# Two FFN weight units multiplied token tile by token tile inside the norm ahead of the FFN

## The reference

```python
        x = x + rms_norm(mix, norm_mix_post[l])
        f = conv_ffn(rms_norm(x, norm_ffn_pre[l]), ffn_up[l], ffn_conv_w[l], ffn_down[l])
        x = x + rms_norm(f, norm_ffn_post[l])
```

## Time and profile before

| what | us |
|---|---|
| median of 3 runs | 2019.67 (2017.91 to 2019.98) |
| profiled execution | 2023.55 |
| its span | 2021.8 |
| PE busy | 1932.9 (96%) |
| DVE busy | 983.6 (49%) |
| ACT busy | 639.9 (32%) |

### The profile page before, as it was taken

How to read it: one execution, slowest core, us unless ns; L and a number is a source line. 1 busy time by engine, 2 the same in 40 slices (tenths; PEclk the granted TensorE clock), 3 DMA queues, 4 the chain that set the end, 5 groups by cost and what they waited for, 6 DMA issues and landing times.

```text
span 2021.8 us, 26669 instructions
## 1 busy us (share of the span) xinstructions
PE 1932.9 (96%) x10902; PEld 1277.9 (63%) x10902; DVE 983.6 (49%) x1678; ACT 639.9 (32%) x1075; POOL 11.4 (1%) x25
## 2 busy tenths in 40 slices
PE   8999999999999999999999999999999899999997
PEld 8979998979998887877996333333333333333332
DVE  6888788888877575488755111111111111111112
ACT  5565556565547333355544000000000000000001
POOL 0000000010000000000000000000000000000000
PEclk9999999999999999999999999999999999999999
DMA  8356654437554640334469999999999999999997
GB/s 336 123 196 221 208 183 178 166 157 260 204 197 153 214 144 34 136 106 166 169 228 363 410 383 434 432 430 432 432 432 432 430 432 432 431 433 431 430 432 304
DMA packets 48225, 592.06 MB, mean 293 GB/s; under 512 B 5696, under 2 KB 6400, under 8 KB 15808
## 3 DMA queue, kind: packets, MB, share of 16 engines
q1 hardware_dynamic: 46080, 584.13, 71.7%
q0 software_dynamic: 1760, 6.33, 1.0%
q10 hardware_dynamic: 288, 0.24, 0.0%
HBM read 589.63 MB, written 1.05 MB: 292 GB/s over the span
## 4 chain that ended last, share of the span: by engine, by line
PE 73%; DMA 19%; DVE 4%; ACT 2%; issue 1%; SPq 0%; DVEq 0%; ACTq 0%
PE psum L2288 46%; PE psum L2737 20%; DMA slots<-exp_w_dram 18%; PE psum L2894 3%; PE psum L2690 3%; DMA work<-exp_w_dram 1%; PE psum L2760 1%; ACT work L1044 0%; DVE work L1609 0%; DMA slots<-w_in_dram 0%; DVE work L1899 0%; DVE split_weights L1554 0%; DVE work L1919 0%; ACT work L1294 0%; DVE split_rows L1514 0%
## 5 line engine op out<-in xcount | busy, mean ns | idle before, releaser
L2737 PE MATMUL psum<-slots,work 128*64 128x512 f32 x2304 | 531.1, 613 | 47.9 <-DMA slots<-exp_w_dram 44.6
L2288 PE MATMUL psum<-split_rows,split_weights 128*128 128x256 f32 (+1 forms) x3888 | 514.1, 294 | 6.7 <-DVE split_rows L1514 3.7
L2288 PEld LDWEIGHTS psum<-split_rows,split_weights 128*128 128x128 f32 x3888 | 493.8, 193 | 28.9 <-issue 9.7
L2737 PEld LDWEIGHTS psum<-slots,work 128*64 128x64 f32 x2304 | 166.3, 140 | 373.5 <-issue 330.4
L2251 DVE TENSOR_SCALAR work<-psum 128x512 f32<-128x512 f32 x32 | 22.1, 692 | 490.9 <-PE psum L2801 490.9
L1535 DVE TENSOR_TENSOR split_weights<-slots,split_weights 128x1024 fp32r<-128x1024 f32 x180 | 219.5, 1223 | 84.6 <-ACT split_weights L1084 83.7
L1084 ACT ACTIVATE split_weights<-slots 128x1024 fp32r<-128x1024 f32 x180 | 190.4, 1062 | 182.3 <-PE psum L2288 161.7
L2288 PE MATMUL psum<-split_weights,split_rows 128*128 128x512 f32 x1008 | 237.0, 395 | 0.0
L2288 PEld LDWEIGHTS psum<-split_weights,split_rows 128*128 128x128 f32 x1008 | 190.1, 190 | 40.9 <-issue 1.7
L1437 ACT ACTIVATE work<-work 128x512 f32<-128x512 f32 x32 | 20.2, 631 | 528.5 <-DVE work L2251 528.5
L2737 PE MATMUL psum<-work 128*64 128x512 f32 x756 | 168.5, 594 | 4.9 <-DMA work<-exp_w_dram 4.7
(11 more groups left out here) (294 smaller groups left out, 1410.0 us busy)
## 6 DMA issues: line engine op xcount, KB each, us to landing
slots<-exp_w_dram SPq DMA_DIRECT2D x65, 4096.0 KB, 29.0
work<-exp_w_dram SPq DMA_DIRECT2D x21, 4096.0 KB, 29.9
slots<-w_in_dram SPq DMA_DIRECT2D x56, 1024.0 KB, 5.1
slots<-ffn_up_dram SPq DMA_DIRECT2D x44, 1024.0 KB, 5.0
cond_work<-ada_wT_dram SPq DMA_DIRECT2D x48, 512.0 KB, 4.4
slots<-ffn_down_dram SPq DMA_DIRECT2D x20, 1024.0 KB, 4.9
slots<-exp_w_dram SPq DMA_DIRECT2D x10, 2048.0 KB, 14.0
slots<-w_out_dram SPq DMA_DIRECT2D x12, 1024.0 KB, 4.8
```

The lines of the kernel that those rows point to most:

```text
L2288: return nc.tensor.matmul(out_, lhsT, rhs, start=first, stop=last)
L2737: return nc.tensor.matmul(b[rows, :], lhs[:, rows], rhs, start=first, stop=last, skip_group_check=True)
```

## The change

In both layers, in the norm ahead of the FFN:

- PE: the five fillers are gone. Between the transposes of tile 0 and of tile 1 stand 24 products of units 24 and 25, for tile 0 alone and the first four k of each unit; behind the transposes of tile 1 come the other 24 of tile 0 and the 48 of tile 1. So 96 products with 128 moving columns take the place of 48 with 256. They wait for the banks of `F` one by one. The unit loop begins with unit 26.
- ACT rounds the rows tile by tile. Three banks of tile 0 are rounded between the two squarings of tile 1, the other five banks after the last root.
- DVE takes the low part of two banks of tile 0 after it added tile 1 to `x` and ahead of its normalising, the other six banks after.
- The wait for the FFN's parameters moves from behind the norm to ahead of it, on both engines.

```diff
@@ -33,6 +33,7 @@
 CAT_AT = XHAT_AT + 2 * 2048
 HALF = 2048
 TILE_ORDER = ((0, 0), (1, 0), (0, 1), (1, 1), (2, 0), (2, 1), (3, 0), (3, 1))
+TILE_BY_TILE = tuple((i, t) for t in range(TT) for i in range(4))
 ROW_SLICES = (4, 5, 6, 7, 8)
 RING = 5
 UNIT = 1024
@@ -1064,9 +1065,9 @@
             def evac(key, l, out_, in_, func=ACT.Copy, **kw):
                 nc.scalar.activation(out_, in_, func, **kw).then_inc(evacuated[bank_of(key)], 1)
 
-            def high_rows(key, l, n, col):
-
-                for i, t in TILE_ORDER:
+            def high_rows(key, l, n, col, order=TILE_ORDER):
+
+                for i, t in order:
                     b = take(act, (key, 4 * t + i), l)
                     for c in (0, 1):
                         k = 2 * i + c
@@ -1170,13 +1171,15 @@
                 nc.scalar.activation(flat(cat_split[:, 0, 2:4, :]), take(act, ("RT", 0), l), ACT.Copy).then_inc(cat_high_ready, 1)
                 split_until(MIX_UNITS + 1)
                 load_root_table()
+                act.wait_ge(ffn_par_loaded, 32 * l + 32)
                 for t in range(TT):
                     for square in (square_of_bank, square_of_sum):
                         square("M", l, t, 0)
                         square("M", l, t, 1)
                         root(t)
-                act.wait_ge(ffn_par_loaded, 32 * l + 32)
-                high_rows("F", l, 4, COL_FFN_PRE)
+                        if t and square is square_of_bank:
+                            high_rows("F", l, 4, COL_FFN_PRE, TILE_BY_TILE[0:3])
+                high_rows("F", l, 4, COL_FFN_PRE, TILE_BY_TILE[3:])
 
                 def first_tap(g, u):
                     if g >= 2 and u == 0:
@@ -1503,9 +1506,9 @@
                                                    in1=x[:, t, cut], op0=ALU.mult, op1=ALU.add
                                                    ).then_inc(evacuated[bank_of((key, 2 * t + half))], 1)
 
-            def low_rows(key, l, n, col):
-
-                for j, (i, t) in enumerate(TILE_ORDER):
+            def low_rows(key, l, n, col, order=TILE_ORDER, begun=0):
+
+                for j, (i, t) in enumerate(order, begun):
                     dve.wait_ge(hT_high_ready, 16 * l + (2 * n + j + 1))
                     b = psum[:, bank_of((key, 4 * t + i)), :]
                     tile = slice(t * P, (t + 1) * P)
@@ -1725,12 +1728,14 @@
                                         cat_split[:, 0, 2:4, :].rearrange("p k t -> p (k t)"), ALU.subtract
                                         ).then_inc(evacuated[bank_of(("RT", 0))], 1)
                 split_until(MIX_UNITS + 1)
+                dve.wait_ge(ffn_par_loaded, 32 * l + 32)
                 for t in range(TT):
                     times_gain("M", mix_row, t, (16 * l + 4 * t + 1, 16 * l + 4 * t + 2))
                     add_to_x(l, 8 * l + 2 * t + 3, "M", t)
+                    if t:
+                        low_rows("F", l, 4, COL_FFN_PRE, TILE_BY_TILE[0:2])
                     normalise_tile(8 * l + 2 * t + 4, t)
-                dve.wait_ge(ffn_par_loaded, 32 * l + 32)
-                low_rows("F", l, 4, COL_FFN_PRE)
+                low_rows("F", l, 4, COL_FFN_PRE, TILE_BY_TILE[2:], 2)
 
                 def later_taps(g, u):
                     b = take(dve, ("U", 2 * g + u), l)
@@ -2995,9 +3000,30 @@
 
                 pe.wait_ge(xhat_tile_ready, 2 * l + 2)
                 turn("F", l, 0)
-                keep_clock(("F", 4), l, 5)
+                first = [[unit_weights(MIX_UNITS + c, v) for v in (0, 1)] for c in (0, 1)]
+
+                def tile_products(c, t, ks):
+
+                    b = psum[:, bank_of(("U", 0)), c * T + t * P:c * T + (t + 1) * P]
+                    for k in ks:
+                        if c == 0 and k % 2 == 0:
+                            after_evacuation(pe, ("F", 4 * t + k // 2), l)
+                        for i, (a, v) in enumerate(PASSES):
+                            ins = nc.tensor.matmul(b, first[c][a][:, k, :], hT_split[:, v, k, t * P:(t + 1) * P],
+                                                   start=c + t + k + i == 0, stop=k == KC - 1 and i == 2,
+                                                   skip_group_check=True)
+                    return ins
+
+                fill(pe, ("U", 0), l)
+                pe.wait_ge(w_split, l * len(UNITS) + MIX_UNITS + 2)
+                for c in (0, 1):
+                    tile_products(c, 0, range(4))
                 pe.wait_ge(xhat_ready, 2 * l + 2)
                 turn("F", l, 1)
+                for c in (0, 1):
+                    tile_products(c, 0, range(4, KC))
+                tile_products(0, 1, range(KC)).then_inc(unit_used, 1)
+                done(tile_products(1, 1, range(KC)), ("U", 0))
                 def context_turned(items):
 
                     pe.wait_ge(ctx_hat_ready, 2)
@@ -3010,7 +3036,7 @@
                                                           ctx_row[:, t, k * P:(k + 1) * P], ident)
                         done(ins, ("CT", i))
 
-                for n in range(MIX_UNITS, len(UNITS) - 2):
+                for n in range(MIX_UNITS + 2, len(UNITS) - 2):
                     slot, j = UNITS[n]
                     kind, g = LAYER_SLOTS[slot]
                     if (l, kind, g) == (DEPTH - 1, "down", 4) and j in (0, 3):
@@ -3022,7 +3048,7 @@
                     if kind == "up":
                         u, c = divmod(j, 2)
                         b = fill(pe, ("U", 2 * g + u), l) if c == 0 else psum[:, bank_of(("U", 2 * g + u)), :]
-                        ins = column_unit(b[:, c * T:(c + 1) * T], wu, "F" if n == MIX_UNITS else None)
+                        ins = column_unit(b[:, c * T:(c + 1) * T], wu)
                         if last:
                             done(ins, ("U", 2 * g + u))
                     else:
```

## The result

The change makes the kernel slower: 2029.03 us (median of 10 runs) against 2017.34 (10 runs), 11.7 us more where 4.6 were forecast. The ratio is 1.0072 with a 95% interval of 1.0045 to 1.0099, that is +9 to +20 us; it goes by the means here, which the highest runs pull up (14.6 us apart). The runs of before lie within 5.3 us. Those of the change lie in three groups: five from 2023.24 to 2025.53, two at 2032.53 and 2034.62, three from 2043.16 to 2044.05. The profiled execution is the one of 2034.62, from the middle group.

The account below looks back on a forecast made before the run. PE was taken as the bound, so unit 26's delay passes on fully: +0.6 us a layer at full clock plus 1.7 for the clock dip, +2.3 a layer, +4.6 in all, median 2024.3 us; range 2017.5 to 2029.4.

Parts of the forecast that it names:

- The steps up to the clock: Layer 0, PE from tile 0's transposes to unit 26 at full clock: 137.96 against 137.37 before, +0.6 us.
- PE's first product: PE behind tile 0's transposes: idle 2.65 us until bank 0's release, first product at 126.46.
- The rows' extra work: ACT and DVE in the norm: tile 1's rows ready about 0.32 us later, but PE is later still, so cost 0.
- The transposes of tile 1: PE, layer 0: they start behind the 24 narrow products, at 129.10 at full clock.
- The narrow product: A 128-column product on PE, set by its weight load: 0.110 us, taken from products with 64 columns.
- The whole sum for full clock: Layer 0, tile 0's transposes to unit 26: 137.96 - 122.72 = 15.24 us.
- The rivals with other prices: Narrow products at stream speed, 0.066 us: -5.5 us in all, chance 0.13; at full 4-byte price, 0.240: +26, chance 0.12.
- the 1.56 us: Kernel before, layer 0: unit 26's delay from an undisturbed 135.81 to 137.37, read as wholly the lowered clock.
- the dip: PE's one idle piece of 2.65 us lowers the clock for 3.4 us, as before: 1.7 us a layer.
- The bound from above: Upper limit on the lowered clock's cost behind PE's gap: 1.7 us a layer.
- the prediction's own signs of being wrong: Profile after: the 72 products under 6 us at full clock, over 15 (full price), or the clock row staying at 1.00.
- this end: Upper end of the range, 2029.4: 0.120 a product and undipped runs before, 4.6 + 2 + 3.1.

Follow-up runs that it names:

- row-order run: Kernel before with ACT and DVE as in the change, PE with its fillers and 256-column products as before: 2017.21 us, ratio 1.0005.
- filled-gap run: The change with four fillers put back between the transposes of tile 0 and the first 24 narrow products: 2019.27 us, ratio 1.0009.
- four narrow units: Kernel before with units 24 to 27 multiplied as 192 products of 128 columns behind both transposes: 2056.09 us, ratio 1.0188.
- six-filler profiles: Kernel before with six fillers instead of five, old row order, run twice: 2015.44 and 2015.82 us, ratios 0.9993 and 0.9992.
- narrow-alone run: Kernel before with units 24 and 25 as 96 products of 128 columns behind both transposes, fillers and row order kept: 2035.38 us, ratio 1.0093.
- half-gap run: The change with two fillers put in the gap between tile 0's transposes and the first narrow products: 2020.18 us, ratio 1.0021.
- open gap with wide products: Kernel before without its five fillers and nothing in their place, units 24 and 25 still 256 columns wide: 2016.97 us, ratio 1.0000.
- half wide: The change with 48 narrow and 24 wide products in place of 96 narrow, gap left open: 2026.37 us, ratio 1.0037.

## Why the prediction was right or wrong

**The steps up to the clock held.** PE's first product came at 126.30 behind 2.69 us of idle time (126.46 and 2.65 in the prediction, with the transposes 0.21 us earlier here). The rows' extra work cost next to nothing: the row-order run is at +0.6 us (-0.8 to +2.8). The transposes of tile 1 went behind the 24 products, at 129.33 at full clock (129.10). The narrow product takes 0.112 us at full clock, where 0.110 was read off the 64-column products. The whole sum for full clock was 15.24 us to unit 26; the filled-gap run has 15.39. The rivals with other prices are out: 0.066 and 0.240 a product, since 192 products in a row at full clock took 0.112 us each (four narrow units, layer 0). The Trainium skill, TensorE: Matmul & The Clock Gate, section Back-to-back issue gap, has about 81 ns for pairs of a weight load and a 128-column product in a stream; the measured 112 ns decides for these products of 4-byte type. One reading was off: of the 1.56 us between an undisturbed 135.81 and 137.37 not all "are the clock". In both six-filler profiles the clock stays at 1.00 and the 48 products still take 6.25 us, so some 1.1 us were the clock and 0.5 the rows.

**The term that failed is the clock's.** The prediction said that the dip lasts "for as long as before (3.4 us)" and bounded it by 0 and 1.7 us a layer. The size was taken from a dip behind which 256-column products stood. With narrow products behind it the clock stayed low for 7 to 27 us in the change, 24 in the narrow-alone run and 44 with four narrow units, and a layer lost up to 13.4 us (11.3 and 2.1), not 2.3. The bound from above was wrong in kind, too: it should have let the low clock last until the wide products come back, which would have put unit 26 at 126.46 + 2 x (10.56 + 0.94) = 149.5, close to the 148.43 of layer 0. One of the prediction's own signs of being wrong came up, 72 products in over 15 us (15.60 in layer 0), but not for the reason it gave: at full clock they take 8.24.

**The median and the range.** The median, 2029.03, lies inside the range, 0.4 us under its upper end of 2029.4, and that is luck: this end was put together from a price of 0.120 a product and a kernel before without dips, not from a long low clock. The groups can be priced, as an estimate, from rows and runs above. Take six fillers (2015.4 to 2015.8, no dip) and add 1.82 us a layer for the change at full clock (15.39 - 13.57). A layer with a low stretch of 3.4 us adds 1.6 (the half-gap run), one of 7 us 3.25 (18.64 - 15.39), a long one 10.5 + 2.1. Two dips of 3.4 us, which is what was forecast, would be 2022 to 2023, just below every run of the change. Two stretches of 7 us give some 2026, near the five lowest runs; a long one and one of 7 us, as in the profiled execution, some 2035 (measured 2034.62); two long ones 2044 to 2045, near the three highest. Only the middle group was profiled, so the reading of the two others rests on this estimate.

**Mechanism.** Shown by the medians against before: open gap with wide products 0.3 us, filled gap with narrow ones 2.6, both together 11.7 with a wide spread. It is the pair that costs. In all five low stretches over 12 us that were profiled, the clock was back 3 to 5.5 us after the wide products began.

**Where the gain was meant to come from.** The products that were moved into the wait are half of 24 wide ones, and the other half still has to come behind the transposes at nearly the same price each. So at full clock the change is 15.39 us to unit 26 against 14.65 with a dip and 13.57 without (the six-filler kernel: unit 26, the 49th product, at 136.18, transposes at 122.61). That is 1.8 us a layer over an undisturbed kernel before, 3.6 in all, and the medians of the filled-gap and six-filler runs are 3.5 to 3.8 apart.

**What stays open.** Why the low clock ended after 7 us in layer 1 of the change and after 3.4 in the half-gap run, but only after 27 in layer 0 of the change; and why the four-unit runs agree. It isn't shown that narrow products ever brought the clock back by themselves: in both short cases it was back within 0.5 us of the start of the 72 narrow products (460.51 and 460.18; 131.91 and 131.42), right behind the transposes of tile 1, and in the five long ones, three of which also have these transposes between their narrow products, it was back on wide products only. What differs between narrow and wide at 1.2 GHz can be read: a narrow product comes every (40.68 - 0.3)/191 = 0.211 us (four narrow units, layer 1) and a wide one every (5.43 - 0.4)/23 = 0.22 (half wide, from 138.48). No run has a third width, or 128 columns without new weights for each product, so what it is in the narrow products that keeps the clock down isn't settled.

## What to carry to other kernels

Don't price a lowered clock by the last dip seen: ask what stands behind the gap. The same clock that was back after 3.4 us on wide products stayed low for up to 44 with narrow ones. Splitting a product in two halves of its columns halved nothing here, where each half loads its own weights: 0.112 us against 0.120 leaves 0.008 us a product to gain from moving half of it into a wait. And where the clock is at stake, fillers are part of the schedule: four of them were worth 9 us here, and one more in the old kernel, with the rows in the new order, perhaps 2.0.

## What was not expected of the hardware

The same 96 products took 10.9 and 20.2 us in two layers of one execution, at a busy share of 100% both times. The granted clock fell behind idle pieces of 1.11 and 0.80 us in both layers of the kernel before, but in one layer only of the narrow-alone and of the four-unit run; behind 1.4 us in one layer of two; behind 2.7 in both layers of both profiles that have such a gap (the change, and half wide with the gap open). In the four-unit run PE without a pause did not bring it back for 40 us while its products had 128 columns; wherever it was still low in these layers when 256-column products began, it was back 2.4 to 5.5 us later. At 1.2 GHz, products of 128 and 256 columns cost the same, 0.21 to 0.22 us.
